# Projection, z and gate weights of a hybrid encoder step as three fp32r products, split in place in the weight ring

## The chip, the cores and the metric

The kernel runs on 1 core of one Trainium2 chip. The metric is the device time of one execution in microseconds (us), as the median of several runs. The engines are named as the profile names them: PE is the matmul engine (PEld its weight loads), DVE, ACT and POOL are VectorE, ScalarE and GpSimd, and SP is the queue that issues most DMAs. `ps` is PSUM. `fp32r` is the number format of a matmul that takes one record where an fp32 matmul takes two.

## What is computed

One inference step of a two-layer encoder trunk over 288 tokens (256 of a prompt, 32 of a sample with its caches). Each layer is a token mixer and then a channel mixer (dense SwiGLU in layer 0, 8 experts in layer 1). The change lies in the token mixer:

```python
def token_mixer(h, past_k, past_v, past_ik, conv_buf, s0, w_in, conv_w, ...):
    qa, ka, va, qi, ki, wi, qkv_b, a_b, b_b, z_b, gates = jnp.split(h @ w_in, SPLIT_POINTS, axis=-1)
    o_a = dsa_attention(qa, qi, wi, k_all, v_all, ik_all, P)     # indexer, top-k keys, softmax
    c, conv_new = causal_conv(qkv_b, conv_buf, conv_w)           # 1536 channels, then silu
    qb, kb, vb = jnp.split(c, (B_QK, 2 * B_QK), axis=-1)         # q and k are l2-normalised
    o_b, s_new = gated_delta_rule(qb, kb, vb, g, beta, s0)
    o_b = o_b * lax.rsqrt(jnp.mean(o_b * o_b, ...) + RMS_EPS) * gnorm_g
    o_b = o_b * jax.nn.silu(z_b)
    g_a, g_b = jnp.split(jax.nn.sigmoid(gates), 2, axis=-1)
    y = (g_a * (o_a @ w_oa) + g_b * (o_b @ w_ob)) @ w_out
```

The width is 1024. Of the columns of `w_in`, `qkv_b` has 1536, `z_b` 512 and the gates 2048: in tiles of 128 output channels that is 12, 4 and 16 per layer.

## The kernel before, in words

Activations lie transposed in `hT`, channels on partitions in 8 tiles of 288 tokens. One output tile of 128 channels is 8 products (one for each k) of a 128x128 weight tile with 128x288 of `hT`.

**Weights.** All weights of the program are a list of units of 1 MB (128x2048 f32), loaded in order by SP into `ring`, which has 6 slots (`RING, SLOT = 6, 2048`, L67). The semaphore `unit_used` counts consumed units; `load_units` (L329) issues unit n when `unit_used` has reached n - 5. A consumer raises it with the first matmul after its last use (`Release.mm`, L348, which is why most matmuls show as L349).

**Two kinds of products.** The projections (`wide` L854, `narrow` L868) and the gates (`gate_products` L696) multiply in fp32 straight from the ring. The output projections, the dense MLP and the experts split each unit: ACT writes the high part in fp32r (`split_high`, L368), DVE the rest (`split_low`, L376), into buffers `wh` and `wl` of their own, the activations are split in the same way, and `product` (L392) adds three fp32r products: high x high, high x low, low x high.

**The block `front`** (L768) has one program per engine, written out by hand. PE runs: key and weight columns (P_KI), four indexer tiles (P_QI), four query tiles (P_QA), KA, VA, then 12 tiles for the convolution (`conv_product`, L880) and 4 z tiles. The indexer's score matmuls (L898, L909) write two PSUM banks that ACT empties (`relus`, L1150); DVE weighs the scores and takes the top 64 keys of each query by 8 rounds of MAX8 and MATCH_REPLACE (`choose`, L1325), for three token tiles. Between the convolution tiles PE runs the attention: `logits` (L919), whose row maxima DVE takes (`maxima`, L1351) and whose exponentials ACT takes (`exps`, L1163), then `turn`, `values`, `turn_out`. DVE runs the convolution (`conv`, L1380), ACT its silu (L1146). POOL squares the silu's results (L835, L837) when 4 and when 8 of them are there; PE sums the squares (L1092) after the first z tile, and turns the last three tokens (L1103) before the last z tile. POOL also builds at the start the masks and the distance table `distr` (L833).

**The block `delta`** (L1485) is the delta rule: 23 rounds of small matmuls (`PREP`) for three token tiles, each emptied by DVE or ACT, then 5 steps over the state (`decayed`, `gained`, `inside`). After each round and step PE runs `fill(n)` (L1560): n of the 128 gate products, 109 of them so, the last 19 at the end. ACT empties the gates (`gates_out`, L715). A block ends for all engines together.

**The block `merge`** then needs the units of `w_oa`, `w_ob` and `w_out`, the first of which is split at the end of `delta`.

Of the kernel before, what the change touches and what calls it, by code (L numbers as in the profile page):

```python
# [11 lines left out]
F32 = mybir.dt.float32  # L12
F32R = mybir.dt.float32r
# [60 lines left out]
def program(nc, A, OUT, upto=99):  # L74
    ctx = ExitStack()
    with ctx:
# [8 lines left out]

        ring = sb("ring", [P, RING * SLOT])
        resid = sb("resid", [P, NT, D])
# [16 lines left out]
        itmp = sb("itmp", [P, 320], I32)  # L104
        adm = sb("adm", [P, 2, SEQ])
        ndist = sb("ndist", [P, NT, PAST + DEC])
# [6 lines left out]
        def layout(*tensors):  # L113
# [7 lines left out]
        cT, arena, zT, slopes, distr, identr, away, slopes4, identr4, _, oaT, obT = layout(  # L121
# [4 lines left out]
            ("pad", [P, OAB0 - CT * CO - B_HEADS * T - ARENA - A_HEADS * P - 2 * NT * (PAST + DEC) - 4 * P]), ("oaT", [P, 4, T]), ("obT", [P, 4, T]))  # L126
# [9 lines left out]
        _, dsm = layout(("below_small", [P, DSM0]), ("dsm", [P, OAB0 - DSM0]))  # L136
# [73 lines left out]
        STORED0 = ARENA - CCH - NT * (A_KV + 1) * HD  # L210
        assert ar.at <= STORED0, (ar.at, STORED0)
        ar.at = STORED0
        lrow = ar(CCH)
# [23 lines left out]
        def project_units(l):  # L237
# [17 lines left out]
            for j in range(2):  # L255
                n = len(units)
                unit((slot(n, (8, 256)), w[:, :, O_Z + 256 * j:O_Z + 256 * j + 256]))
# [3 lines left out]
        def merge_units(l):  # L261
            w, ob, wo = rows(A["w_in"][l]), rows(A["w_ob"][l]), rows(A["w_out"][l])
            n0 = len(units)
            for j in range(4):
                c = 256 * j
                n = len(units)
                unit((slot(n, (8, 256)), w[:, :, O_GA + c:O_GA + c + 256]))
                n = len(units)
                unit((slot(n, (8, 256)), w[:, :, O_GB + c:O_GB + c + 256]))
            for j in range(4):  # L270
# [32 lines left out]
        N_PROJ, N_GATE, N_MERGE, N_FFN, N_EXP = 14, 8, 8, 3 * D_FF // 256, 3 * D_FFE // 256  # L303
# [39 lines left out]
        class Release:  # L343

            def __init__(self):
                self.due = None

            def mm(self, *a, **k):  # L348
                ins = nc.tensor.matmul(*a, **k)  # L349
                if self.due:  # L350
                    ins.then_inc(self.due, 1)
                    self.due = None
# [39 lines left out]
        def product(out, terms):  # L392
# [4 lines left out]
            return ins  # L397

# [82 lines left out]
        def masks(pool):  # L481
# [52 lines left out]
            for i in range(NT):  # L534
                c.link(nc.gpsimd.iota(itmp[:, 0:PAST + DEC], pattern=[[1, PAST + DEC]], base=-TILES[i][0],
                                      channel_multiplier=-1))
                c.link(nc.gpsimd.tensor_copy(ndist[:, i, :], itmp[:, 0:PAST + DEC]))
# [2154 lines left out]
```

## Time and profile before

| | |
|---|---|
| median of 3 runs | 2016.28 us |
| lowest and highest run | 2013.37 and 2016.62 us |
| the profiled execution | 2013.88 us, its span 2012.2 us |
| PE, PEld busy | 97%, 81% of the span |
| DVE, ACT, POOL busy | 67%, 53%, 4% |
| layer 0: `front`, `delta` | 22 to 177 us, 177 to 307 us |
| layer 1: `front`, `delta` | 599 to 754 us, 754 to 884 us |
| the experts | 950 us to the end |

The span is cut into records, one for each instruction on each engine. A fp32 matmul leaves two records, an fp32r matmul one. A record's own length is modelled and overlaps with the next, so rates are taken from start to start. Rows of the timeline give start and length in us, then the engine, the line of the source, what is written and read, and the count; in brackets stands the idle time ahead of it and who ended it. PEclk is the granted PE clock as a share of full speed.

### The profile page before, as it was taken

The page shows a single profiled execution, that of the slowest core. Times are in us where ns is not written, and L with a number is a line of the kernel's source. Part 1 is how long each engine was busy: PE and PEld are TensorE (multiplying, and loading weights), DVE is VectorE, ACT ScalarE, POOL GpSimd, SP SyncE. Part 2 cuts the span into 40 slices and gives each one's busy share as a digit, 9 for nine tenths or more (in the row PEclk, how much of TensorE's full clock was granted, in tenths as well). Part 3 has the DMA queues.
Part 4 walks back from the last instruction along what each step waited for, and adds up shares of the span by engine and source line. Part 5 has one row for each costly group of instructions (what it writes and reads, how often), then busy time and mean ns, then how long its engine had stood idle before and what let it go on. Part 6 is the DMA issues. An engine that isn't in the chain of part 4 may idle for free. (4 is left out here: it accounts for less than half of the span.)

```text
span 2012.2 us, 25990 instructions
## 1 busy us (share of the span) xinstructions
PE 1952.5 (97%) x10605; PEld 1633.7 (81%) x10605; DVE 1351.8 (67%) x1547; ACT 1063.1 (53%) x1206; POOL 82.3 (4%) x152
## 2 busy tenths in 40 slices
PE   6999999999999999999999999999999999999995
PEld 5677889899986778888888788888888888888884
DVE  3744237644434643265797988879889798897986
ACT  2233234444332324244776776767767677676773
POOL 4003000100011011001000000000000000000000
PEclk9999999999999999999999999999999999999998
DMA  7223226354433232143599999999999999999992
GB/s 207 84 71 111 64 67 194 127 161 161 148 92 96 74 111 81 51 157 127 205 371 321 354 357 318 373 328 346 362 314 370 329 350 364 310 374 335 339 371 108
DMA packets 260480, 456.91 MB, mean 227 GB/s; under 512 B 32218, under 2 KB 111274, under 8 KB 260356
## 3 DMA queue, kind: packets, MB, share of 16 engines
q1 hardware_dynamic: 258966, 454.74, 65.9%
q8 instruction: 87, 1.43, 0.3%
q10 hardware_dynamic: 1390, 0.44, 0.1%
q14 instruction: 37, 0.30, 0.0%
HBM read 452.11 MB, written 3.04 MB: 226 GB/s over the span
## 5 line engine op out<-in xcount | busy, mean ns | idle before, releaser
L380 DVE TENSOR_TENSOR wl<-ring,wh 128x2048 fp32r<-128x2048 f32 x385 | 880.4, 2289 | 245.3 <-ACT wh L374 242.0
L374 ACT ACTIVATE wh<-ring 128x2048 fp32r<-128x2048 f32 x385 | 737.2, 1917 | 320.5 <-PE ps L349 320.5
L349 PE MATMUL ps<-hT,ring 128*128 128x288 f32 (+1 forms) x1376 | 358.9, 412 | 3.6 <-ACT tanhs L722 1.7
L349 PE MATMUL ps<-wh,xgh 128*128 128x512 f32 x896 | 354.5, 396 | 2.4 <-DVE wl L380 2.4
L349 PE MATMUL ps<-wh,xgl 128*128 128x512 f32 x896 | 349.6, 390 | 0.0
L349 PE MATMUL ps<-wl,xgh 128*128 128x512 f32 x896 | 349.3, 390 | 0.0
L349 PEld LDWEIGHTS ps<-hT,ring 128*128 128x128 f32 (+1 forms) x1376 | 251.7, 189 | 78.5 <-issue 6.5
L349 PEld LDWEIGHTS ps<-wh,xgh 128*128 128x128 f32 x896 | 168.3, 188 | 40.1 <-DVE wl L380 5.7
L349 PEld LDWEIGHTS ps<-wh,xgl 128*128 128x128 f32 x896 | 168.2, 188 | 36.0
L349 PEld LDWEIGHTS ps<-wl,xgh 128*128 128x128 f32 x896 | 168.4, 188 | 33.4
L349 PE MATMUL ps<-wh,gEh 128*128 128x512 f32 x448 | 143.4, 401 | 0.0
L349 PE MATMUL ps<-wl,gEh 128*128 128x512 f32 x448 | 139.6, 393 | 0.0
L349 PE MATMUL ps<-wh,gEl 128*128 128x512 f32 x448 | 138.1, 389 | 0.0
L349 PE MATMUL ps<-hTh,wh 128*128 128x288 f32 x352 | 103.3, 296 | 0.4 <-ACT hTh L666 0.4
L349 PE MATMUL ps<-hTh,wl 128*128 128x288 f32 x352 | 102.6, 294 | 0.0
L349 PE MATMUL ps<-hTl,wh 128*128 128x288 f32 x352 | 99.6, 296 | 0.6 <-DVE hTl L2177 0.6
L349 PEld LDWEIGHTS ps<-wh,gEl 128*128 128x128 f32 x448 | 84.1, 188 | 19.3
L349 PEld LDWEIGHTS ps<-wl,gEh 128*128 128x128 f32 x448 | 84.1, 188 | 18.9
L349 PEld LDWEIGHTS ps<-wh,gEh 128*128 128x128 f32 x448 | 78.9, 189 | 12.0
L1757 ACT ACTIVATE arena<-ps 128x512 f32<-128x512 f32 (+1 forms) x72 | 32.4, 491 | 103.7 <-PE ps L1574 67.8
L1574 PEld LDWEIGHTS ps<-arena 128*128 128x128 f32 (+1 forms) x672 | 64.3, 163 | 6.4
L349 PEld LDWEIGHTS ps<-hTh,wh 128*128 128x128 f32 x352 | 66.0, 187 | 1.2 <-issue 1.2
(407 smaller groups left out, 2408.5 us busy)
## 6 DMA issues: line engine op xcount, KB each, us to landing
ring<-in_moe_w SPq DMA_DIRECT2D x336, 1024.0 KB, 5.4
ring<-in_w_in SPq DMA_DIRECT2D x38, 1024.0 KB, 5.2
ring<-in_ffn_w SPq DMA_DIRECT2D x33, 1024.0 KB, 5.2
ring<-in_w_out SPq DMA_DIRECT2D x8, 1024.0 KB, 5.3
ring<-in_w_in SPq DMA_DIRECT2D x32, 128.0 KB, 3.0
ring<-in_w_oa SPq DMA_DIRECT2D x16, 256.0 KB, 3.9
ring<-in_w_ob SPq DMA_DIRECT2D x8, 512.0 KB, 5.0
resid<-in_x_prompt SPq DMA_DIRECT2D x1, 1024.0 KB, 5.4
```

Source lines behind the costliest of these rows:

```text
L349: ins = nc.tensor.matmul(*a, **k)
L374: nc.scalar.activation(wh[:, k % WS, :], ring[:, s:s + SLOT], ACT.Copy).then_inc(hi_ready, 1)
L380: ins = nc.vector.tensor_tensor(wl[:, k % WS, :], ring[:, s:s + SLOT], wh[:, k % WS, :].bitcast(F32), ALU.subtract)
L1574: return nc.tensor.matmul(v4(b, n, ww)[:, h, :], d[lhs][0:n, h, :], d[rhs][0:n, h, :], start=True, stop=True)
L1757: nc.scalar.activation(tl[i][dst][0:n], v4(bank(r, i), n, BD if r == "u" else n), ACT.Copy).then_inc(prep_act, 1)
```

## The change

The products of the convolution, z and gate tiles become three fp32r products. Each of their weight units now takes two ring slots: the unit is loaded into the first; ACT writes its high part into the second, and DVE writes the low part over the loaded unit, in the first. This is a pair; there are 16 in a layer (6 convolution, 2 z, 8 gates). The empty second slot is a unit without a load, so that the ring holds 3 pairs. The activations are split once per layer into `hPh` (ACT, 128x2304) and `hPl` (DVE, in five pieces).

```diff
-            for j in range(6):
+            for j in range(8):
                 n = len(units)
-                unit((slot(n, (8, 256)), w[:, :, O_CV + 256 * j:O_CV + 256 * j + 256]))
...
+                unit((slot(n, (8, 256)), w[:, :, c:c + 256]))
+                unit()
...
-        N_PROJ, N_GATE, N_MERGE, N_FFN, N_EXP = 14, 8, 8, 3 * D_FF // 256, 3 * D_FFE // 256
+        N_PROJ, N_GATE, N_MERGE, N_FFN, N_EXP = 22, 16, 8, 3 * D_FF // 256, 3 * D_FFE // 256
...
+        def pair_high(act, l, j):
+
+            n = pair_unit(l, j)
+            have(act, n)
+            act.wait_ge(unit_used, n + 2 - RING)
+            w, h, _ = pair_slots(l, j)
+            nc.scalar.activation(h, w, ACT.Copy).then_inc(ph_ready, 1)
...
+        def pair_low(dve, l, j):
+
+            dve.wait_ge(ph_ready, N_PAIR * l + j + 1)
+            w, h, r = pair_slots(l, j)
+            nc.vector.tensor_tensor(r, w, h.bitcast(F32), ALU.subtract).then_inc(pl_ready, 1)
+
+        def pair_terms(l, j, k, c):
+
+            _, h, r = [x.rearrange("p (a b) -> p a b", a=KD)[:, k, P * c:P * c + P] for x in pair_slots(l, j)]
+            return (h, hPh[:, k, :]), (h, hPl[k]), (r, hPh[:, k, :])
```

`pair_low_half` does the same for half a unit; the second half raises `pl_ready`. The gates, and with them the place of ACT's work for a pair two further on:

```diff
                 if k == 0 and q % 2 == 0:
-                    have(pe, n)
+                    pe.wait_ge(pl_ready, N_PAIR * l + j + 1)
...
-                ins = rel.mm(gate_bank(q)[:, 0:T], slot(n, (8, 256))[:, k, P * (q % 2):P * (q % 2) + P], hT[:, k, :],
-                             start=(k == 0), stop=(k == KD - 1))
+                for i, (x, y) in enumerate(pair_terms(l, j, k, q % 2)):
+                    ins = rel.mm(gate_bank(q)[:, 0:T], x, y, start=(k == 0 and i == 0), stop=(k == KD - 1 and i == 2))
...
+                if q % 2 == 0 and GATE_PAIR + q // 2 + 2 < N_PAIR:
+                    pair_high(act, l, GATE_PAIR + q // 2 + 2)
```

On DVE the first low part for the gates stands in two halves behind the `ktok` round, the next around `vtok`, then one half behind each of X2, X3, Y1 and TT, two behind `grown(0)` and `vnew(2)`, and two behind `vnew(3)`.

In `front`, the indexer's scores go to four PSUM banks and start before the first query tile instead of behind it, and the first logits stand behind four convolution tiles instead of two:

```diff
                     def it_room(k):
-                        if k >= 2:
+                        if k >= 10:
                             pe.wait_ge(it_read, l * NTURN + k - 1)
+                        elif k >= 4:
+                            pe.wait_ge(it_read, l * NTURN + k - 3)
...
                     indexer(0)
+                    wide(P_QA, u0 + 3, 0)
+                    indexer(1)
                     wide(P_QA + 1, u0 + 3, 1)
-                    indexer(1)
...
                     conv_product(1)
+                    conv_product(2)
+                    conv_product(3)
                     pe.wait_ge(new_evac, 3 * (l + 1))
                     pe.wait_ge(pen_ready, l + 1)
                     logits(0, 0)
-                    conv_product(2)
+                    conv_product(4)
                     logits(0, 2)
-                    conv_product(3)
+                    conv_product(5)
```

POOL builds `distr` in both layers now, through the tile `away`, because the stored distances and other tiles gave their room to the split activations:

```diff
+                    for i in range(NT):
+                        c.link(nc.gpsimd.iota(itmp[:], pattern=[[1, PAST + DEC]], base=-TILES[i][0], channel_multiplier=-1))
+                        c.link(nc.gpsimd.tensor_copy(away[:, i, :], itmp[:]))
+                    c.link(nc.gpsimd.tensor_scalar(distr[:], away[:].bitcast(F32), 0.0, 2.0, ALU.min, ALU.mult))
+                    nc.gpsimd.tensor_tensor(distr[:], distr[:].bitcast(F32), away[:].bitcast(F32), ALU.subtract).then_inc(pen_ready, 1)
```

**Place A.** PE in `front`, behind the fourth indexer tile. L1035 to L1037 (now L1099 to L1101) are the decays, L898 and L909 (now L965 and L976) the scores, L916 (now L983) the sample's score sum, L349 (now L359) the projections. Before:

```order
L1037 MATMUL ps<-dsm,ones 128x8
L898 MATMUL ps<-arena 128x256 x8
L349 MATMUL ps<-hT,ring 128x288 x8
L898 MATMUL ps<-arena 128x256 x8
L909 MATMUL ps<-arena 128x288 x2
L349 MATMUL ps<-hT,ring 128x288 x8
L916 MATMUL ps<-arena 32x288 x2
```

Now:

```order
L1101 MATMUL ps<-dsm,ones 128x8
L965 MATMUL ps<-arena 128x256 x8
L359 MATMUL ps<-hT,ring 128x288 x8
L965 MATMUL ps<-arena 128x256 x8
L359 MATMUL ps<-hT,ring 128x288 x8
L976 MATMUL ps<-arena 128x288 x2
L359 MATMUL ps<-hT,ring 128x288 x8
L983 MATMUL ps<-arena 32x288 x2
```

The first query tile, which stood ahead of the decays, now stands between the two groups of scores, and another tile ahead of the sample's.

**Place B.** DVE in `front`, behind the last `choose`. L1349 (now L1431) writes its result, L1355 (now L1437) takes the maxima of the logits, L1386 and L1388 (now L1468 and L1470) are the convolution, L441 is the low part of a pair. Before:

```order
L1349 TENSOR_SCALAR away<-arena 32x288
L1355 TENSOR_REDUCE arena<-ps 128x2 x2
L1386 TENSOR_SCALAR cT<-arena 128x291
L1388 SCALAR_TENSOR_TENSOR cT<-arena,cT 128x291 x3
L1394 COPY arena<-arena 128x3
L1395 COPY arena<-arena 128x3
L1355 TENSOR_REDUCE arena<-ps 128x2 x2
```

Now:

```order
L1431 TENSOR_SCALAR away<-arena 32x288
L1437 TENSOR_REDUCE arena<-ps 128x2 x2
L441 TENSOR_TENSOR ringr<-ring,ringr 128x2048
L1468 TENSOR_SCALAR cT<-arena 128x291
L1470 SCALAR_TENSOR_TENSOR cT<-arena,cT 128x291 x3
L1476 COPY arena<-arena 128x3
L1477 COPY arena<-arena 128x3
L1437 TENSOR_REDUCE arena<-ps 128x2 x2
```

The low part of the third pair stands behind the first maxima.

**Place C.** ACT in `front`, near its end. L1119 and L1120 (now L1185 and L1186) empty a convolution tile, L1196 (now L1262) the sample's attention output, L1148 (now L1214) is silu, L1143 (now L1209) empties a z tile, L427 is the high part of a pair. Before:

```order
L1196 ACTIVATE oaT<-ps 128x4x32
L1148 ACT_TABLE_LOAD
L1148 ACTIVATE cT<-cT 128x291 x6
L1119 ACTIVATE arena<-ps 128x256
L1120 ACTIVATE arena<-ps 128x32
L1148 ACTIVATE cT<-cT 128x291 x2
L1119 ACTIVATE arena<-ps 128x256
L1120 ACTIVATE arena<-ps 128x32
L1148 ACTIVATE cT<-cT 128x291
L1143 ACTIVATE zT<-ps 128x288
```

Now:

```order
L1185 ACTIVATE arena<-ps 128x256
L1186 ACTIVATE arena<-ps 128x32
L1262 ACTIVATE oaT<-ps 128x4x32
L1214 ACT_TABLE_LOAD
L1214 ACTIVATE cT<-cT 128x291 x9
L1209 ACTIVATE zT<-ps 128x288
L427 ACTIVATE ringr<-ring 128x2048
L1214 ACTIVATE cT<-cT 128x291 x2
```

Before, two convolution tiles were emptied behind the start of silu; now the twelfth is emptied ahead of it.

## Rows read from the trace of the kernel before

**Rows 1.** Page, part 1: busy us (share of the span), records.

```profile
PE 1952.5 (97%) x10605; PEld 1633.7 (81%) x10605; DVE 1351.8 (67%) x1547; ACT 1063.1 (53%) x1206; POOL 82.3 (4%) x152
```

**Rows 2.** Timeline, PE, layer 0: a run of fp32 products and what follows.

```profile
31.46 15.69 PE L349 MATMUL ps<-hT,ring 128*128 128x288 f32 x64
46.99 0.28 PE L1035 MATMUL ps<-dsm,cumU 128*128 128x4 f32 x2
```

**Rows 3.** Windows: stretch, length, busy us by engine (records), PEclk, DMA, GB/s.

```profile
450.00:500.00 50.00, 50.00 (x377) 50.00 (x377) 24.14 (x23) 20.89 (x24) 0.00 (x0) 1.00 0.52 169
52.00:54.00 2.00, 2.00 (x9) 1.15 (x7) 0.52 (x2) 0.68 (x2) 0.00 (x0) 0.50 0.00 0
```

**Rows 4.** Timeline, PE, layer 1: the indexer's scores.

```profile
627.05 1.13 PE L898 MATMUL ps<-arena 64*128 64x256 f32 x8
629.45 1.13 PE L898 MATMUL ps<-arena 64*128 64x256 f32 x8 [1.26 <-ACT arena L1154]
630.51 4.15 PE L349 MATMUL ps<-hT,ring 128*128 128x288 f32 x16
...
639.35 0.76 PE L909 MATMUL ps<-arena 64*128 64x288 f32 x4 [1.23 <-ACT arena L1154]
```

**Rows 5.** Timeline, PE, layer 0: the same place.

```profile
51.24 2.08 PE L898 MATMUL ps<-arena 64*128 64x256 f32 x8 [1.26 <-ACT arena L1154]
53.24 4.72 PE L349 MATMUL ps<-hT,ring 128*128 128x288 f32 x16
```

**Rows 6.** Page, parts 5 and 6: split of a unit, and loads of `w_in`.

```profile
L380 DVE TENSOR_TENSOR wl<-ring,wh 128x2048 fp32r<-128x2048 f32 x385 | 880.4, 2289 | 245.3 <-ACT wh L374 242.0
L374 ACT ACTIVATE wh<-ring 128x2048 fp32r<-128x2048 f32 x385 | 737.2, 1917 | 320.5 <-PE ps L349 320.5
...
ring<-in_w_in SPq DMA_DIRECT2D x38, 1024.0 KB, 5.2
```

**Rows 7.** Timeline, DVE, layer 0: the last `choose` ends, first maxima.

```profile
90.89 0.30 DVE L1349 TENSOR_SCALAR away<-arena 32x288 fp32r<-32x288 f32 x1
91.75 1.29 DVE L1355 TENSOR_REDUCE arena<-ps 128x2 f32<-128x512 f32 x2 [0.56 <-PE ps L938]
```

**Rows 8.** Timeline, ACT, layer 0: silu starts.

```profile
148.21 1.28 ACT L1148 ACT_TABLE_LOAD   x1
149.50 2.12 ACT L1148 ACTIVATE cT<-cT 128x291 f32<-128x291 f32 x6
```

**Rows 9.** Timeline, POOL, layer 0: the squares and what follows them.

```profile
151.04 2.13 POOL L835 TENSOR_TENSOR arena<-cT 128x1164 f32<-128x1164 f32 x1 [104.49 <-ACT cT L1148]
153.12 2.19 POOL L837 TENSOR_TENSOR arena<-cT 128x1164 f32<-128x1164 f32 x1
```

**Rows 10.** Timeline, PE, layer 0: the end of `front`.

```profile
147.46 11.81 PE L349 MATMUL ps<-hT,ring 128*128 128x288 f32 x48
159.19 4.10 PE L1092 MATMUL ps<-arena,sel 128*8 128x291 f32 x16
...
172.84 4.05 PE L349 MATMUL ps<-hT,ring 128*128 128x288 f32 x16
```

**Rows 11.** Timeline, DVE, layer 0: the convolution beside POOL; the last copies of `front`.

```profile
153.37 4.70 DVE L1388 SCALAR_TENSOR_TENSOR cT<-arena,cT 128x291 f32<-128x291 f32 x3
...
172.16 1.87 DVE L1429 COPY arena<-ps 6x512 f32<-6x512 f32 x3 [4.00 <-PE ps L1103]
```

**Rows 12.** Timeline, PE, layer 0: the last 19 gate products and the end of `delta`.

```profile
294.05 5.60 PE L349 MATMUL ps<-hT,ring 128*128 128x288 f32 x22
300.52 4.15 PE L349 MATMUL ps<-hT,ring 128*128 128x288 f32 x16 [0.87 <-ACT tanhs L722]
```

**Rows 13.** Timeline, ACT, layer 0: what stands ahead of the tanh that this waits for.

```profile
298.27 1.89 ACT L374 ACTIVATE wh<-ring 128x2048 fp32r<-128x2048 f32 x1
300.07 0.69 ACT L722 ACTIVATE tanhs<-ps 128x288 f32<-128x288 f32 x2
```

**Rows 14.** Timeline, DVE, layer 0: a step over the state.

```profile
287.21 1.12 DVE L1895 SCALAR_TENSOR_TENSOR arena<-arena,dsm,ps 128x128 f32<-128x128 f32 x4 [2.28 <-PE ps L1670]
```

More of the change, by code:

```diff
@@ L83, in program @@
         ps = [ctx.enter_context(nc.psum_tensor(f"ps{b}", [P, 512], F32)) for b in range(8)]
+        with ExitStack() as mem:
+            ringr = mem.enter_context(nc.sbuf_tensor("ringr", [P, RING * SLOT], F32R))
         ring = sb("ring", [P, RING * SLOT])
+        with ExitStack() as mem:
+            hPh = mem.enter_context(nc.sbuf_tensor("hPh", [P, KD, T], F32R))
+            hPl01 = mem.enter_context(nc.sbuf_tensor("hPl01", [P, 2, T], F32R))
         resid = sb("resid", [P, NT, D])
@@ L1213, in _ @@
                     ins.then_inc(wi_ready, 1)
+                    nc.scalar.activation(hPh[:], hT[:], ACT.Copy).then_inc(hph_ready, 1)
                     evac(P_QI + 1)
@@ L1245, in _ @@
                     exps_sample()
-                    evac(P_CV + 6)
-                    evac(P_CV + 7)
+                    evac(P_CV + 8)
+                    pair_high(act, l, 6)
+                    evac(P_CV + 9)
                     turned_sample()
                     outs(1)
-                    evac(P_CV + 8)
-                    evac(P_CV + 9)
+                    evac(P_CV + 10)
+                    pair_high(act, l, 7)
+                    evac(P_CV + 11)
                     outs(2)
-                    for j in range(0, 6):
+                    for j in range(0, 9):
                         silu(j)
-                    evac(P_CV + 10)
-                    silu(6)
-                    silu(7)
-                    evac(P_CV + 11)
-                    silu(8)
                     evac(P_Z)
+                    pair_high(act, l, 8)
                     silu(9)
+                    silu(10)
                     evac(P_Z + 1)
-                    silu(10)
                     silu(11)
                     evac(P_Z + 2)
+                    pair_high(act, l, 9)
                     evac(P_Z + 3)
@@ L1304, in _ @@
                     nc.vector.tensor_scalar(sp_[:, 0, :, :], sp_[:, 0, :, :], 0.0, None, ALU.max).then_inc(sm_dve, 1)
+                    dve.wait_ge(hph_ready, l + 1)
+                    for k, n, low in ((0, 2, hPl01), (2, 3, hPl24), (5, 1, hPl5), (6, 1, hPl6), (7, 1, hPl7)):
+                        nc.vector.tensor_tensor(low[:], hT[:, k:k + n, :], hPh[:, k:k + n, :].bitcast(F32), ALU.subtract
+                                                ).then_inc(hpl_ready, 1)
                     dve.wait_ge(sm_act, l + 1)
@@ L1413, in _ @@
                     conv(5)
+                    pair_low(dve, l, 5)
+                    conv(6)
                     normalise(1)
-                    conv(6)
+                    conv(7)
+                    pair_low(dve, l, 6)
+                    conv(8)
                     normalise_sample()
-                    for j in range(7, CT):
+                    conv(9)
+                    pair_low(dve, l, 7)
+                    for j in range(10, CT):
                         ins = conv(j)
@@ L2232, in moe @@
         def moe():
[L2233 removed]
+            iu = flag
             with nc.Block() as block:
```

180 lines of the change are left out of this document (114 added, 66 removed).

## The prediction

> **What bounds the kernel now.** The page's first part comes first: PE is busy 97% of the span, the next engine is DVE with 67% [rows 1]. Read with the two blocks that the change touches, this says that PE's own work sets the time: in `front` and `delta` the waits of PE add up to a few us. So the second view is PE's timeline, for the rate of each kind of matmul and for the few gaps in brackets. The third is the timelines of DVE, ACT and POOL at the places where the new splits go, since they must now stay ahead of a faster PE.
>
> **The products.** 64 records of fp32 products start 15.53 us (46.99 - 31.46) ahead of the next work [rows 2]: 0.2427 us a record, 0.4853 us a product. Where the dense MLP runs three fp32r products of the same 128x288 shape, 377 records take 50 us at full clock [rows 3]: 0.1326 us each, 0.3979 us for three. A product thus gains 0.0874 us. 32 output tiles of 8 products in 2 layers are 512 products: **44.8 us** gained, 22.4 in a layer, of which 11.2 lie in `front` and 11.2 in `delta`. All of it is on PE. The rate for three comes from high and low parts of weights and activations in the same roles, so I take it whole; the bounds are no gain (were the mix no faster than fp32) and 44.8.
>
> The Trainium skill, "FP8 and Floating Point Precision", section "TensorE Precision Notes", says that a true fp32 product is four passes of the array. If three fp32r products were three of these passes, a quarter of 0.4853 us would go, and 512 products would gain 62.1 us instead of 44.8. The rows speak against it: three measured 0.3979 us, which is 82% of the fp32 product and not 75%.
>
> **The indexer.** With two banks PE waited 1.26, 1.26 and 1.23 us in a layer for ACT to empty them [rows 4]. With four banks, and a query tile between the groups [place A], ACT has 3.9 us for 2.2 us of work, so all three waits go: 3.8 us a layer. In layer 0 this place ran also at half clock: granted 0.50 from 52 to 54 us [rows 3], and the scores and the tile behind took 2.08 and 4.72 us [rows 5] against 1.13 and 4.15 in layer 1 [rows 4], 1.5 us more. With the waits ahead of it gone I let it go as well (bounds 0 and 1.5). Together 2 x 3.8 + 1.5 = **9.1 us**. Gross gain: 44.8 + 9.1 = 53.9 us.
>
> **The splits in `front`.** A pair costs ACT 1.92 us and DVE 2.29 us [rows 6]; 8 pairs by the time `front`'s products need them, and two more for the gates. A pair j + 3 can be loaded only when PE has released pair j: 5.2 us to land [rows 6], 1.9 and 2.3 to split, some 0.4 for the hand-overs, 9.9 us. Two pairs are 4 x 3.18 = 12.7 us of PE, more with the attention between, so this chain has at least 2.8 us to spare. The places that have not are these:
> 1. The third pair's low part stands on DVE behind `maxima(0,0,2)` [place B], which waits for PE's first logits, and PE's next work is the fifth convolution tile, which needs that low part. PE waits 1.29 + 2.29 us and two hand-overs of 0.1 [rows 6, 7]: 3.7 us a layer. Whether `choose` ends early or late doesn't matter: it now ends near 88 us instead of 91.2 [rows 7], ahead of the logits.
> 2. This delays the release of the second pair, so ACT gets the fifth pair's load late, and the exponentials behind it: PE waits 0.4 us in `turn(0)`.
> 3. Near the end, ACT can start silu only when the twelfth convolution tile and `turn_out_sample` are done [place C]. Then come emptying (0.7), the table load 1.28 and four silu of 0.355 [rows 8], 3.4 us, and POOL's two squares, 2.13 + 2.19 us [rows 9]: 7.9 us with the hand-overs until PE may sum them. Ahead of the sum PE has one z tile. Before, it had three tiles, 48 records in 11.8 us [rows 10], and no wait. Now it has 3.2 us and waits 4.7 us. The last convolution tiles also run on DVE while POOL works, where three instructions took 4.70 us [rows 11]; that ends ahead of its readers.
> 4. The last pair for the gates: its load waits for the second z tile, its low part stands behind DVE's copies of the turned rows. DVE copies 1.87 us [rows 11], then 2.29: some 4.6 us from the turning on, while PE's last tile, 3.9 us before [rows 10], takes 3.2 and its emptying 0.4. The block ends with DVE, 1.6 us late with the later load counted.
> That is 3.7 + 0.4 + 4.7 + 1.6 = 10.4 us a layer. `hPh` (some 2.1 us of ACT) and `hPl` (some 2.7 us of DVE) fall in idle time ahead of the decays. POOL's table takes some 9 us longer, priced by its own cast and tensor rates, and ends near 52 us, ahead of its first reader near 59; against layer 0's `choose` it may cost DVE up to 5 us, which DVE can lose before PE waits more than 1 us.
>
> **`delta`.** Each of 109 fills gets 0.087 us shorter, the cover of each round's emptying with it, 0.26 us at most where PE showed no wait and had over 1 us to spare. The half splits of 1.2 us stand behind the sums that PE wants and 5 us ahead of the next. Only the two behind `vnew(3)` collide: 2.3 us in a gap of 2.28 us [rows 14], and with the shorter fill the state is 0.4 us late. In the tail PE waited 0.87 us for a tanh [rows 12] that stands behind ACT's first merge split and its chain [rows 13]. That tanh doesn't move, PE comes 1 us earlier, and waits that longer; what is left of the tail's 1.66 us is some 0.95. Loss 0.4 + 0.7 = 1.1 us a layer. The merge units come later in the ring, released inside the last 19 fills, but are read over 10 us later.
>
> **The sum.** Losses 2 x (10.4 + 1.1) = 23.0 us. 53.9 - 23.0 = 30.9 us. The profiled execution took 2013.88 us, which gives 1983.0 us; the median shown is 2.4 us higher, and of the three runs one lies near the profiled one. I put the forecast 1 us up: **1984 us**.
>
> **The rivals.**
> - *The losses are hidden.* If DVE and ACT reach the four places sooner than I place them, most of the 23 us go, and the gross gain stays: 2014 - 50 = 1964 us. For it: the engines are half idle there. Against: places 1 and 3 follow from the order alone. 14%.
> - *The new gaps cost clock.* Each of the four long waits of PE (two in a layer) may be followed by a spell at half clock as in layer 0 [rows 3, 5]. The spell there cost 1.5 us; from that to twice that, 4 x (1.5 to 3) = 6 to 12 us, or 8 in the middle: 1992 us. For it: those waits are three times as long as the 1.26 us there. Against: layer 1 had the same waits and kept its clock. 22%. The Trainium skill, "TensorE: Matmul & The Clock Gate", section "HAM oscillation — how this bites in real kernels", says that gaps of PE in a loop can throttle its clock each time; by that rule all four spells come, and the sum would be the 1992 us of this rival.
> - *Three quarters.* The passes of the quoted rule would give 17 us more than my rate, 1967 us. Against it is the measured rate. 2%.
> - *Slower: the ring is too shallow.* With 3 pairs in it, 26 refills pass through SP, DMA, ACT and DVE, in order on each. The chain has 2.8 us to spare beside the plain tiles. Should a load land 2.8 + 1.2 = 4.0 us later than the 5.2, at 9.2 us, each refill costs 1.2 us and the 30.9 us are gone; at 10.7 us to landing each costs 2.7, 70 us in all: 2053 us. Against: nothing in these stretches loads the DMA engines but these same units, one at a time. 4%.
> - *The products don't get faster*, because weights from the ring in fp32r run at another rate than from `wh`. At the fp32 rate 44.8 us go: 2028 us. Against: place and type of the data are of the same kind. 2%.
> The likeliest case keeps 56%.
>
> **How the numbers follow.** The range goes from 1966 (nearly all losses hidden) to 1998: the clock's 12 us, and a few us for DVE beside POOL and for rounds whose cover was thinner than I read. A measurement of this kernel can tell about 0.2%, 4 us, from no change. Only the last two rivals and part of what is unnamed give no gain: faster 0.92, same 0.02, slower 0.06.
>
> **What would show it.** In the changed profile: 24 records per tile at 0.133 us each; no wait on ACT's relu at the scores; PE waiting some 3.7 us on a low part behind the first logits, and some 4.7 us on POOL's squares; blocks `front` near 6 us shorter in layer 0 and near 5 us in layer 1, `delta` near 10 us each. It is wrong if PE waits in many places for low parts or loads, if PEclk falls behind the new gaps, or if the three products take over 0.41 us.

## The result, and the profile after

The changed kernel took 2000.63 us, the median of 4 runs (1998.07 to 2005.28), the kernel before 2015.97 beside it; the ratio is 0.9928, with a 95% interval of 0.9915 to 0.9941. It is faster, as forecast, but by about 15 us and not by 31: above the range of 1966 to 1998. The profiled execution is the slowest of the four, 2005.28 us with a span of 2003.6, so it has somewhat more of what cost the time than the median has. The forecast for it was 1983.0 us: 22.3 us have to be found.

The page's first part, which answers to [rows 1], and the mean granted clock of the core, of after and then of before:

```profile
PE 1926.7 (96%) x11117; PEld 1664.5 (83%) x11117; DVE 1434.1 (72%) x1600; ACT 1127.7 (56%) x1240; POOL 99.6 (5%) x160
```

```profile
core 0: 2003.6 us, clock 0.981
```

```profile
core 0: 2012.2 us, clock 0.992
```

PE still sets the time. The clock row is the first clue: a mean of 0.981 means 0.019 x 2003.6 = 38 us of full-speed time not granted, before it was 0.008 x 2012.2 = 16 us. The difference is 22 us (the last digit of the two means leaves it some 2 us either way; clock that falls in idle time counts here too, though it costs nothing).

PE's waits in the changed kernel, in total, times and the longest of them in us:

```profile
PE ps L1158 <- POOL arena L885: 9.3, 2, 4.8
...
PE ps L359 <- DVE mv L2134: 7.9, 2, 4.3
...
PE ps L359 <- DVE ringr L441: 6.9, 2, 3.4
PE ps L1687 <- PEq L840: 4.3, 2, 2.2
PE ps L359 <- ACT tanhs L767: 3.6, 2, 1.8
```

From the top: the sum of squares (forecast 4.7 us in each layer); the start of the merge stage, which waits for the end of `delta` (1.55 us a layer before, here 3.59 and 4.28; not forecast); the low part ahead of the fifth convolution tile (forecast 3.7 a layer); the end of `front` (0.76 before, 2.17 and 2.10 here; forecast 1.6 more); the tanh (0.87 before [rows 12], 1.80 here). The waits on ACT's relu of [rows 4] are gone.

Now the clock. Windows of PE in the changed kernel (stretch, length, PE busy with its records, PEclk, DMA share, GB/s), in pairs of a wait and what follows it: ahead of and in the fifth convolution tile, ahead of and in the sum, the start of `delta`, the start of the merge stage, and in layer 1 a place among the steps of `delta`.

```profile
91.60:95.00 3.40, 0.01 (x1) 0.84 0.00 0
95.00:97.00 2.00, 1.95 (x8) 0.50 0.10 13
97.00:101.00 4.00, 4.00 (x20) 0.53 0.78 256
...
151.20:156.00 4.80, 0.02 (x1) 0.94 0.34 118
156.00:160.00 4.00, 3.93 (x11) 0.65 0.00 0
...
175.00:186.00 11.00, 10.82 (x48) 0.54 0.40 120
186.00:260.00 74.00, 74.00 (x666) 1.00 0.19 58
302.00:304.50 2.50, 2.50 (x12) 0.53 1.10 358
...
841.40:844.60 3.20, 3.20 (x18) 0.51 0.00 0
```

Behind each wait PE is busy nearly throughout and its clock is at or near 0.50, the lower of its two levels (1.2 GHz), where before it was at 1.00 (the window with 0.65 holds the end of such a stretch as well). The same shows in the durations. The timeline of PE (start and duration in us, what runs, and in brackets the idle time ahead and who ended it) at the sum and at the start of `delta`, after:

```profile
156.07 5.43 PE L1158 MATMUL ps<-arena,sel 128*8 128x291 f32 x16 [4.84 <-POOL arena L885]
```

```profile
175.18 4.98 PE L1687 MATMUL ps<-arena,ones 128*128 128x128 f32 x24 [2.17 <-PEq L840]
```

and before, where the sum stands in [rows 10] with 4.10 us, the start of `delta`:

```profile
177.64 3.03 PE L1592 MATMUL ps<-arena,ones 128*128 128x128 f32 x24 [0.76 <-PEq L794]
180.60 4.15 PE L349 MATMUL ps<-hT,ring 128*128 128x288 f32 x16
```

What each slow stretch costs, by the start of its work to the start of the next, against the same work at the full clock: the fifth convolution tile 5.9 and 6.0 us against 3.2 (2.7 and 2.8; the runs in which this tile had no wait later showed 3.30 for it, so these two are 0.1 us high each); the sum 5.4 and 5.7 against 4.0 (1.3 and 1.6); the first two groups of `delta` 4.9 + 5.9 and 4.6 + 4.7 against 3.0 + 3.3 (4.6 and 3.1); the steps of `delta` in layer 1, 1.5; the start of the merge stage 0.9 in each layer, by the time from there to the start of layer 1 and of the mixture stage in either kernel. Together 19.4 us. With the late end of `delta`, (3.59 - 1.55) + (4.28 - 1.55) = 4.8 us, that makes 24.2 us, and the forecast's own losses came out 1.4 us smaller (their account is below): 22.8 us for the 22.3 missing. That is a sum from one execution, and its closeness is partly luck, since each term is read to some 0.1 us only; the runs below test its causes.

### The profile page after: what moved, and what is told of

It reads as the page before. It is cut to its first block and busy times, and to the rows that moved or that the text cites. A ratio compares the mean times of both kernels' runs of the same rounds, so it can differ in the third digit from the quotient of the medians.

```text
span 2003.6 us, 27175 instructions
## 1 busy us (share of the span) xinstructions
PE 1926.7 (96%) x11117; PEld 1664.5 (83%) x11117; DVE 1434.1 (72%) x1600; ACT 1127.7 (56%) x1240; POOL 99.6 (5%) x160
## 5 line engine op out<-in xcount | busy, mean ns | idle before, releaser
L359 PE MATMUL ps<-wh,xgh 128*128 128x512 f32 x896 | 354.4, 396 | 2.4 <-DVE wl L390 2.4
L359 PE MATMUL ps<-wh,xgl 128*128 128x512 f32 x896 | 349.4, 390 | 0.0
L359 PE MATMUL ps<-wl,xgh 128*128 128x512 f32 x896 | 349.1, 390 | 0.0
L359 PE MATMUL ps<-hPh,ringr 128*128 128x288 f32 x1024 | 237.3, 313 | 10.5 <-DVE ringr L441 6.9
L359 PEld LDWEIGHTS ps<-wh,xgh 128*128 128x128 f32 x896 | 168.3, 188 | 39.9 <-DVE wl L390 5.8
L359 PEld LDWEIGHTS ps<-wh,xgl 128*128 128x128 f32 x896 | 168.2, 188 | 35.8
L359 PEld LDWEIGHTS ps<-wl,xgh 128*128 128x128 f32 x896 | 168.5, 188 | 33.1
L359 PEld LDWEIGHTS ps<-hPh,ringr 128*128 128x128 f32 x1024 | 177.2, 196 | 16.9 <-issue 9.6
L359 PE MATMUL ps<-hPl,ringr 128*128 128x288 f32 x512 | 155.8, 304 | 0.0
L359 PE MATMUL ps<-wh,gEh 128*128 128x512 f32 x448 | 143.4, 401 | 0.0
L359 PE MATMUL ps<-wl,gEh 128*128 128x512 f32 x448 | 139.6, 393 | 0.0
L359 PE MATMUL ps<-wh,gEl 128*128 128x512 f32 x448 | 138.1, 390 | 0.0
L359 PE MATMUL ps<-hTh,wh 128*128 128x288 f32 x352 | 103.3, 296 | 0.4 <-ACT hTh L711 0.4
L359 PE MATMUL ps<-hTh,wl 128*128 128x288 f32 x352 | 102.6, 294 | 0.0
L359 PEld LDWEIGHTS ps<-hPl,ringr 128*128 128x128 f32 x512 | 101.0, 197 | 0.1
L359 PE MATMUL ps<-hTl,wh 128*128 128x288 f32 x352 | 99.7, 296 | 0.6 <-DVE hTl L2283 0.6
L359 PEld LDWEIGHTS ps<-wh,gEl 128*128 128x128 f32 x448 | 84.1, 188 | 19.3
L359 PEld LDWEIGHTS ps<-wl,gEh 128*128 128x128 f32 x448 | 84.0, 188 | 18.9
L359 PE MATMUL ps<-hT,ring 128*128 128x288 f32 (+1 forms) x352 | 89.2, 410 | 1.9 <-PEq L594 0.9
L359 PEld LDWEIGHTS ps<-wh,gEh 128*128 128x128 f32 x448 | 78.9, 189 | 12.0
```

## The experiments

All were timed in three rounds (e11_tanhgap in five) beside the kernel before, whose median was 2013.9 to 2014.4 us there. Times are medians, to be held against the 2000.6 us of the changed kernel, which was itself timed beside the kernel before (2015.97 there). The kernel before thus lay 1.6 to 2.1 us lower in these rounds, so differences of under some 3 us from the changed kernel are not told apart by the medians.

### Idle products in the gaps, first try

```diff
+        def warm_up(bank, times):
+            for _ in range(times):
+                nc.tensor.matmul(bank[:, 0:256], ident[:], ident[:].unsqueeze(1).to_broadcast([P, 2, P]), start=True, stop=True)
...
                     logits(0, 2)
+                    warm_up(ps[7], 6)
                     conv_product(5)
...
                     z_product(0)
+                    warm_up(ps[6], 8)
                     pe.wait_ge(sq_ready, 2 * (l + 1))
...
                     z_product(3)
+                    warm_up(ps[6], 4)
```

and six more into `ps[5]` behind the last transposes of `delta`.

> The changed kernel with matrix products of identity matrices added on TensorE, whose results nobody reads, in four gaps of each layer: six ahead of conv tile 5 (gap 3.44 us), eight ahead of the sum of squares (4.84), four behind the last z tile (2.17) and six at the end of the delta stage (3.59 and 4.28). Each is 256 columns of fp32 and should take 0.49 us at the full clock, so that each group is about as long as its gap or a little shorter. Theory 1 (the gaps themselves cost what I priced, and the rest of the missing gain went to stretches at half the clock that follow them): the gaps stay as long, the granted clock stays at 1.00 behind them, conv tile 5 takes 3.2 us instead of 5.9, the sum's 16 records 4.0 instead of 5.4, the first two groups of the delta stage 3.0 and 3.3 instead of 4.9 and 5.9; the spell inside the delta steps at 841 may stay. In all 15 to 20 us less than the changed kernel: 1981 to 1986 us. Theory 2 (the longer times behind the gaps are waits for data or weights, and the clock only goes along with them): the added products fill the gaps but the tiles behind stay as long, 1996 to 2004 us.

Measured 1996.7 us, ratio 0.991 (0.9892 to 0.9927). I had put the first group in the wrong place: `conv_product(5)` counts from 0 and is the sixth tile; the wait stands ahead of `conv_product(4)`. So this wait stayed, 2.4 us a layer of useless work came behind it, and the fifth tile was still slow (4.9 us in both layers, where the changed kernel had 5.9 and 6.0). Where the products did stand in a gap, theory 1 came out: the sum took 4.03 us in both layers and the first group of `delta` 2.96 in both. Six of these products took 2.4 us in a row, 0.40 us each, and ten take 0.43 each in the next run; the 0.49 us of the expectations was too high. The windows of PE in the fifth tile, then at the sum, then through the start of `delta`:

```profile
95.00:101.00 6.00, 6.00 (x34) 0.72 0.56 175
...
157.00:162.00 5.00, 4.67 (x21) 1.00 0.02 3
162.00:186.00 24.00, 23.55 (x183) 1.00 0.33 101
```

### Idle products in the gaps, in the right place

```diff
                     logits(0, 0)
+                    warm_up(ps[7], 6)
                     conv_product(4)
```

with ten ahead of the sum, four at the end of `front`, five at the end of `delta`.

> The changed kernel with products of identity matrices that nobody reads (256 columns of fp32, 0.49 us each), now six of them ahead of the fifth conv tile, where TensorE waits 3.44 us (in e1_warm they stood one tile later, where it doesn't wait, and cost 2 x 2.4 us), ten ahead of the sum of squares, four behind the last z tile and five at the end of the delta stage. The waits stay, the idle time doesn't. Theory 1 (half clock follows from idle gaps): the granted clock is at 1.00 from 60 to 310 us, conv tile 5 takes 3.2 us instead of 5.9 and 6.0; against e1_warm 4.9 us for the misplaced group and 5.5 us for the tiles less: profiled 1983 us, median 1984 to 1988. Theory 2 (tile 5 is slow for another reason than the clock): 1989 to 1992.

Measured 1986.53 us, ratio 0.9867 (0.9845 to 0.989), 14 us below the changed kernel, though every engine does the same work in the same order and PE has 50 products more, some 21 us of them, that nobody reads. The fifth tile took 3.35 us in both layers. Windows of PE:

```profile
60.00:300.00 240.00, 234.09 (x1760) 1.00 0.33 97
640.00:830.00 190.00, 187.50 (x1470) 1.00 0.25 76
```

What makes tile 5, the sum and the start of `delta` slow is thus the clock that follows PE's idle time, and not data or weights that come late.

### Silu earlier

```diff
                     pe.wait_ge(sums_read, l + 1)
+                    pe.wait_ge(oa_ready, l * NT + 3)
...
                     evac(P_CV + 8)
+                    for j in range(0, 4):
+                        silu(j)
                     pair_high(act, l, 6)
                     evac(P_CV + 9)
+                    for j in range(4, 8):
+                        silu(j)
...
-                    for j in range(0, 9):
-                        silu(j)
+                    silu(8)
```

> The changed kernel with ScalarE's silu of conv tiles 0 to 3 moved from behind the twelfth tile's copy to behind the ninth's, and of tiles 4 to 7 to behind the tenth's, so that GpSimd squares them while TensorE still has three tiles to do. Theory 1 (the gap plus a half-clock spell behind it): the 4.84 and 4.49 us waits ahead of the sum go, and the spells behind them too (1.4 + 1.7 us): 12.4 us less, 1988 us (1986 to 1991). Theory 2 (gap alone costs, the slow stretch behind it is something else): 9.3 less, 1991 us. Theory 3 (GpSimd's squares stretch VectorE's conv taps wherever they run: 5.79 us for three taps instead of 1.64 beside them in the profile of after; moved forward they delay the low parts of the next pairs): a new wait of up to 4 us a layer for a low part, 8 us less of the gain, 1996 us.

Measured 1981.35 us, ratio 0.9836 (0.9817 to 0.9855): 19 us less, more than the 12.4 of theory 1. The wait ahead of the sum is gone and no new one came in its place (the added wait of PE, ahead of turning the sums, shows no idle time), so theory 3 falls: GpSimd's squares do stretch VectorE's work where they now run (a copy of 0.16 us took 2.12), but VectorE has that time there. The rest of the 19 us is the start of `delta`. It ran at the full clock in both layers, although the wait ahead of it was as long as ever:

```profile
167.62 3.03 PE L1691 MATMUL ps<-arena,ones 128*128 128x128 f32 x24 [2.40 <-PEq L840]
```

```profile
168.00:178.00 10.00, 10.00 (x85) 1.00 0.45 134
730.00:740.00 10.00, 9.98 (x83) 1.00 0.46 134
```

9.3 us of wait, 2.9 for the sum, 7.7 for `delta`'s start are 19.9 us. The medians are 19.3 us apart, but these terms come from the two profiled executions, and those are 24.3 us apart. Most of the rest is 3.3 us less of wait at the start of the merge stage (4.6 in all for 7.9), 1.0 less in the fifth tile of layer 0 and 1.5 less in the steps of `delta` in layer 1, against 1.5 more for a slow last gate tile in layer 0. None of these stands where the edit does.

### The third pair's low part earlier

```diff
-                    maxima(0, 0, 2)
                     pair_low(dve, l, 2)
+                    maxima(0, 0, 2)
```

> The changed kernel with VectorE's low part of pair 2 ahead of the first two maxima instead of behind them. Theory 1: the wait of 3.44 and 3.43 us ahead of conv tile 5 goes, and so does the half-clock spell behind it (tile 5 in 3.2 us instead of 5.9 and 6.0): 2 x (3.4 + 2.7) = 12.3 us less, 1988 us; the maxima come 2.3 us later, and a wait of up to 1 us a layer may come at turn(0), then 1990. Theory 2 (the slow tile isn't the clock's): 6.9 us less, 1994 us.

Measured 1987.15 us, ratio 0.9869 (0.9846 to 0.9893): 13.5 us less, theory 1 (12.3). The clock stayed at 1.00 to 100 us. What this simple account misses shows behind the sum, whose 4.85 and 4.56 us of wait are still there: its records now took 6.46 and 6.87 us, 1 us more than in the changed kernel, and the start of `delta` was at the full clock in both layers.

```profile
60.00:100.00 40.00, 40.00 (x243) 1.00 0.26 80
150.00:157.00 7.00, 6.92 (x19) 0.64 0.00 0
170.00:180.00 10.00, 9.68 (x81) 1.00 0.43 134
```

The clock that follows a wait can thus be paid for at another place behind it than in the changed kernel.

### State stores ahead of two merge units

```diff
-                    load_units(sp, first["gate", l] + N_GATE - 2)
+                    load_units(sp, first["gate", l] + N_GATE - 4)
                     sp.wait_ge(s_ready, NQ * (l + 1))
```

> The changed kernel in which SyncE issues only the loads of the first two merge units ahead of its wait for the final states and of the two state stores, and the other two behind the stores. Theory 1 (the delta stage ends late because the state stores stand in the queues behind 2 MB of weights): the wait at the end of the delta stage falls from 3.59 and 4.28 us to the 1.55 of the kernel before, and with it the half-clock stretch at the start of the merge stage: 4.8 + 2 to 3 us less, 1993 to 1994 us. Theory 2 (the stage ends with VectorE's last tile whatever the stores do): under 1 us less, 2000 us; and the weights that come later may make the merge stage wait for its third unit, then 2001 to 2003.

SyncE's timeline at the end of `delta` in layer 0, in the changed kernel and then in this one (start, duration of the issue, what is issued):

```profile
288.59 1.26 SPq L347 DMA_DIRECT2D ring<-in_w_oa  x2
...
291.85 0.60 SPq L347 DMA_DIRECT2D ring<-in_w_ob  x1
292.50 0.51 SPq L1626 DMA_DIRECT2D out_new_gdn_p<-arena  x1
293.04 1.16 SPq L1627 DMA_DIRECT2D out_new_gdn_s<-arena  x1
```

```profile
290.10 0.39 SPq L1626 DMA_DIRECT2D out_new_gdn_p<-arena  x1
290.53 0.51 SPq L1627 DMA_DIRECT2D out_new_gdn_s<-arena  x1
291.09 1.28 SPq L347 DMA_DIRECT2D ring<-in_w_oa  x2
```

and PE's wait at the start of the merge stage here, which was 7.9 us with a longest of 4.3:

```profile
PE ps L359 <- DVE mv L2134: 3.1, 2, 1.5
```

The cause of the late end is shown: with the stores 2.4 us earlier and nothing in front of them, the waits are 1.55 and 1.54 us, as in the kernel before. One rival has to be set aside for it, since this wait was short also in kernels that kept SyncE's order, as in e9_sumgap (described below):

```profile
PE ps L359 <- DVE mv L2140: 3.1, 2, 1.5
```

In both layers of e9_sumgap the last gate tile was slow (4.8 us), so PE came 1.5 us later and had that much less to wait (3.59 - 1.5 = 2.1 us; for the other 0.5 us no run shows a cause). Of the layers whose last gate tile ran at the full clock, and which have no idle products there, the three with the old order waited 3.59, 4.28 and 3.06 us (layer 1 of e2_silu), the four with the stores ahead 1.55 (layer 0 here), 1.58 (layer 1 of e8_low9) and 1.55 twice (e11_tanhgap). In layer 1 here the tile was slow, so that layer alone would show only part of it. Measured 1998.02 us, ratio 0.9904 (0.9881 to 0.9926), 2.6 us less where 7 to 8 were expected. Of the two slow starts of the merge stage one is left (0.57 from 869 to 873 us in layer 1), and in layer 1 the last gate tile was slow (4.83 us for 3.29) and the sum's records took 6.98 us for 5.65. The executions of both kernels differ by 6 to 7 us among themselves, and by the ratios (0.9904 against 0.9928) the gain is nearer 5 us than 3, so its size isn't settled by this run.

### The three together, and one more

e5_all has the three edits above. e8_low9 has them and

```diff
                     c.link(V.tensor_scalar(s2, s2, 1.0 / BD, None, ALU.mult))
+                    pair_low(dve, l, 9)
```

with that call taken from the end of `front`.

> The changed kernel with three reorderings together: silu of conv tiles 0 to 7 earlier (as in e2_silu), low part of pair 2 ahead of the first maxima (as in e3_low), state stores ahead of the last two merge units (as in e4_store). Theory 1 (each gap costs itself and a half-clock stretch that follows it, here or at the next gap): e2_silu took 19 us off, e3_low 13, e4_store 3; the stretch at the start of the delta stage went in e2_silu and in e3_low, so it counts once (4.6 us): 30 us less than the changed kernel, 1970 us (1964 to 1974), with the granted clock at 1.00 from 60 to 260 us. Theory 2 (the work that was moved only changes places, and the next wait takes over): no better than e2_silu, 1978 to 1982.

> As e5_all, and VectorE's low part of pair 9 moved from the end of the front into the start of the delta stage, where VectorE waits 4.87 us. Theory 1: the front ends with the wait of before (0.76 us instead of 2.2), 2 x 1.4 = 2.8 us less than e5_all. Theory 2 (another engine or a store ends the front as late): no difference from e5_all, within 0.5 us.

Measured 1972.57 us, ratio 0.9792 (0.9776 to 0.9808), for the first and 1967.7, ratio 0.9772 (0.9756 to 0.9788), for the second. The waits for the squares and for `ringr` are off the list in both, and the wait at the end of `front` fell as expected from 4.5 us in all to 1.5. The remaining difference, 4.9 us instead of 2.8, is again the clock: in e5_all the start of `delta` in layer 0 was slow behind its 2.33 us wait (0.84 from 163 to 173 us), in e8_low9 it wasn't. In e8_low9, of the two `delta` stages the one in layer 0 still shows a spell, behind the tanh wait, and another at the start of the merge stage (0.50 from 284 to 286 us):

```profile
60.00:260.00 200.00, 198.22 (x1527) 1.00 0.25 78
276.00:280.00 4.00, 4.00 (x21) 0.57 1.03 247
720.00:834.00 114.00, 112.20 (x950) 1.00 0.31 90
```

### Which gap slows the start of `delta`

Only one group of idle products each: ten ahead of the sum (e9_sumgap), four at the end of `front` (e10_frontgap).

> The changed kernel with idle products in one gap only: ten ahead of the sum of squares, behind the first z tile. The waits ahead of conv tile 5 (3.44 us) and at the end of the front (2.17) stay as they are. Question: which gap the slow start of the delta stage (4.9 and 5.9 us for its first two groups instead of 3.0 and 3.3) belongs to. Theory A (the two gaps together: one wait of 4.84 and one of 2.17 us with 12 us between): with the first one filled the sum's records take 4.03 us, the delta stage starts at the full clock, and 2 x (1.5 + 4) = 8 to 11 us less than the changed kernel, 1990 to 1992 us. Theory B (the 2.17 us wait alone does it): only the sum's own slow records go, 3 us less, 1997 us.

> The changed kernel with idle products in another single gap: four at the end of the front, behind the last z tile. Theory A (the two gaps together make the slow start of the delta stage): filling the second one also brings the delta stage's first groups to 3.0 and 3.3 us in most executions, while the sum's records stay at 5.4 us: 5 to 8 us less than the changed kernel, 1993 to 1996 us. Theory B (the 2.17 us wait alone): the same here, and e9_sumgap tells them apart. Theory C (the long wait of 4.84 us alone, with a delay): the start of the delta stage stays slow, 1999 to 2001 us.

e9_sumgap measured 1989.6 us, ratio 0.9874 (0.9859 to 0.9889); e10_frontgap 1997.04, ratio 0.9908 (0.9892 to 0.9923). Windows of PE at the sum, then at the start of `delta`, of the first and of the second:

```profile
154.00:159.00 5.00, 4.62 (x20) 1.00 0.01 3
172.00:182.00 10.00, 9.74 (x81) 1.00 0.45 134
738.00:748.00 10.00, 9.99 (x83) 1.00 0.46 134
```

```profile
156.00:164.00 8.00, 7.41 (x20) 0.60 0.00 0
177.00:187.00 10.00, 9.66 (x80) 1.00 0.44 134
```

Filling the wait ahead of the sum also mends the start of `delta`, with its own wait (2.25 us) untouched: 11 us, as theory A has it, and theory B falls as the only cause. Filling the second wait mends `delta`'s start too, but gives only 3.6 us, below theory A's 5 to 8: the sum's records took 6.85 us in layer 0, more than the 5.4 of the changed kernel, as in e3_low. Over all profiled executions with a wait of 2.1 to 2.4 us at the end of `front`, 12 layers in all, the start of `delta` was slow in 4 and not in 8; with the wait filled or cut to 0.76 it was slow in none of 10. The wait at the end of `front` was there in all four slow cases; the wait ahead of the sum in three of them. Alone the first sufficed once (e5_all), and both together didn't always (e3_low, and layer 1 of e4_store). One pattern shows in the six layers that had both waits: in the three where the sum's records took 5.4 to 5.7 us, `delta`'s start was slow, and in the three where they took 6.5 to 7.0 (both layers of e3_low, layer 1 of e4_store), it wasn't. The loss thus fell either behind the sum alone, or partly there and mostly behind the second wait. What decides in a single case stays open.

### The tanh

```diff
-                    fill(2 * KD * KD)
+                    fill(2 * KD * KD - KD - filled[0])
+                    warm_up(ps[5], 3)
+                    fill(KD)
```

on top of e8_low9.

> As e8_low9, with three idle products behind the last gate tile but one, where TensorE waits 1.80 us for a tanh (0.87 in the kernel before) and where e8_low9 shows half the clock at 276.5 to 280 us in the first layer. Theory 1 (the doubled wait brings the spell): the last gate tile takes 3.3 us in both layers instead of 4.8 in the first, 1.5 us less, 1964 to 1966 us. Theory 2 (the spell comes from the whole stretch of short products): it appears as before, or earlier in the delta steps, 1967 to 1968 us.

Measured 1963.69 us, ratio 0.9745 (0.9732 to 0.9758): theory 1, though the gain over e8_low9 (4 us) is larger than the 1.5 of the one spell that it aimed at. The profiled executions are 2.2 us apart, and there the slow start of the merge stage, some 0.9 us, went as well; the slower two executions of e8_low9 had a lower mean clock than its profiled one (0.988 against 0.991). In the ten other kernels with the 1.80 us wait here (the changed one among them), the last gate tile was slow in 13 of 20 layers, though in neither layer of the changed kernel's profiled execution; in this kernel in neither. The five times lie between 1963.06 and 1964.01 us. The spread between executions goes with the granted clock. The changed kernel's slower two had a mean of 0.981 and its faster two 0.983, some 4 us of full-speed time; in e7_warm2 the four lie 8.8 us apart and their means run from 0.994 to 0.990, 8 us. Which stretches made it isn't shown, since one execution of each kernel was profiled.

```profile
60.00:310.00 250.00, 246.15 (x1879) 1.00 0.37 111
645.00:835.00 190.00, 186.14 (x1483) 1.00 0.33 94
```

```profile
core 0: 1961.3 us, clock 0.993
```

It beats both kernels: 2.5% under the kernel before, 1.8% under the changed one.

### The indexer alone

The kernel before with four banks, the scores a tile earlier and ACT's copies in that order:

```diff
-                return ps[3 + k % 2][:, :]
+                return ps[3 + (k % 4 if k < 10 else k % 2)][:, :]
...
                     indexer(0)
+                    wide(P_QA, u0 + 3, 0)
+                    indexer(1)
                     wide(P_QA + 1, u0 + 3, 1)
-                    indexer(1)
```

> The kernel before with the indexer's part of the change alone: four banks for the score turns, the scores one tile earlier, ScalarE's copies in that order. No fp32r products. By the priced waits (3.8 us a layer and 1.5 us of half clock in the first): 7.6 to 9.1 us less than the kernel before, 2006 us; if VectorE's choice or the decay factors become late instead, a gain of under 3 us, 2012.

Measured 2004.94 us, ratio 0.9954 (0.9937 to 0.997), 9.3 us less than the 2014.28 beside it (6.0 to 12.7 by the interval); forecast 9.1. PE waits for no relu any more, and the half clock of [rows 3] at 52 us is gone:

```profile
48.00:56.00 8.00, 8.00 (x42) 1.00 0.43 134
```

## Why the prediction was off

**What was right.** The direction; the products: a tile of 24 records takes 3.19 to 3.22 us from its start to the next work's (0.133 us a record, forecast 0.1326) against 3.88 before, and a `delta` stage without a slow stretch takes 116.95 us to its last transposes (e11_tanhgap, e1_warm) against 126.86, 9.9 us less where 11.2 - 1.1 = 10.1 was forecast; the indexer, 9.3 for 9.1. The quarter of the product's time that the rule on four passes would save did not come. The places and sizes of the waits in `front` also hold: 3.44 and 3.43 for 3.7, 4.84 and 4.49 for 4.7, 1.4 more at its end for 1.6, and 0.9 more at the tanh for 0.7. Of the 0.4 us in `turn(0)` nothing shows as long as tile 5 is late; with that cured it is there (3.4 to 3.7 us for the sixth tile in e3_low, e5_all and e8_low9 instead of 3.2). The ring kept up: no wait for a load.

**The step that failed: the clock was a rival at 22% and belonged in the sum.** I had the mechanism with "Each of the four long waits of PE (two in a layer) may be followed by a spell at half clock", and against it "layer 1 had the same waits and kept its clock". Two things were wrong in it. The evidence against was from waits of 1.26 us [rows 4], and I let it speak for waits three and four times as long. All 12 waits of 3.4 us that the profiles show at the fifth tile were followed by a slow tile; none of the two that were filled was. And the price was for four spells of 1.5 to 3 us, since I counted only the two long waits of a layer: there were nine slow stretches, with 19.4 us in all, of 0.9 to 4.6 us. The dearest stood behind the third wait of the layer, the one at the end of `front`, which I had priced at its 1.6 us and left out of the rival, as I did the tanh and the end of `delta`. Where the rival had 6 to 12 us it would have needed 19.

The Trainium skill, "TensorE: Matmul & The Clock Gate", section "HAM oscillation — how this bites in real kernels", says that a kernel whose matrix products come in groups with waits between can find the clock lowered at the start of each group. This case agrees at the fifth tile, 12 times of 12, and with 4 of 12 at the start of `delta` it shows that a shorter wait may or may not do the same.

**The step that was missing: a store behind the loads.** I wrote of the merge units that they are "released inside the last 19 fills, but are read over 10 us later", and looked at who reads them and not at what is queued behind them. SyncE issues them just ahead of the state stores whose landing the block waits for: 2.0 and 2.7 us. With the stores ahead the wait was 1.55 to 1.58 us, as before the change, in all four layers in which no slow tile shortened it. The change leaves SyncE's order there as it was; it only lets two of its loads run later, and the stores behind them with them.

**The balance.** 1983.0 + 19.4 (slow stretches) + 4.8 (stores) - 1.8 (waits in `front` over-priced: 0.5 at tile 5, 0.1 at the sum, 0.8 in `turn(0)`, 0.4 at the end) + 0.4 (`delta`, 9.9 for 10.1 in each layer) = 2005.8 us; the profiled execution took 2005.28. With the waits repaired instead of only warmed over, the same products and indexer give 1963.7 us, the time of the rival "the losses are hidden" (1964). That kernel also has reordered work and idle products, so the agreement to 0.3 us is in part luck, but the gain that the change could give was read rightly in the main; what it gave was decided by some 13 us of waits in each layer and by what followed them.

**Open.** Why the slow stretch behind the sum was longer in four layers (6.5 to 7.0 us for its records instead of 5.4 to 5.7). It isn't that another wait had been taken away or filled, for in layer 1 of e4_store none had. What lets the wait at the end of `front` pass 8 times in 12 is open too. In layer 1 of the changed kernel the stretch at 841 us has no wait of PE ahead of it that the profile lists, nor has one at 835 us, at the same place of `delta`, in e10_frontgap: not every slow stretch is explained by a wait.

## To carry to other kernels

When PE's work gets shorter, list every wait that opens, the short ones too, and price each as itself plus a stretch of half speed behind it; here ten useless products in one gap of each layer gave back 11 us, more than the 9.3 us of the gap itself. A mean granted clock that differs between executions of one kernel, and goes along with their times, is a sign of the same; a small spread is no sign that the waits are gone (e9_sumgap has the 3.4 us wait in both layers and a spread of 0.9 us). For every load that becomes possible at another time, look down its queue for a store that somebody waits for.

## What the runs showed of the chip

- A wait of 3.4 us of PE was followed by 4.9 to 6.0 us for a tile of 3.2 us each time (12 of 12), one of 2.1 to 2.4 us by a slow start in 4 of 12, one of 1.80 us by a slow tile in 13 of 20, and the 0.76 us at the end of `front` by one in none of 8 (the kernel before, e6_indexer, e8_low9, e11_tanhgap). The waits of 4.5 to 4.9 us ahead of the sum were followed by slow records in 8 of 8 (5.4 to 7.0 us instead of 4.03).
- What ran ahead of a wait may count too, though no run was made to test it. A wait of 1.54 to 1.68 us at the start of the merge stage was followed by a slow start in 7 of 10 layers in which the gate tile just ahead of it had been slow, and in none of 8 in which that tile had run at the full clock.
- The slow stretch may come late: behind the 4.84 us wait the sum's records took 1.3 us too long, and the stage that began 19 us after it another 4.6 us, which went when the first wait was filled (e9_sumgap).
- Idle products of 0.40 to 0.43 us each, reading and writing what nobody uses, hold the clock at 1.00 through a wait.
- Three fp32r products of 128x288 take 0.40 us from ring slots as from the split buffers, 82% of one fp32 product of 0.485 us.
- Three taps of VectorE's convolution took 5.79 us beside GpSimd's squares in layer 0 of the changed kernel, and 1.64 us without them.
